# Moving the difference attention of a transformer's last layer between the products of that layer's projections

## The chip, the cores and the metric

The kernel runs on one core of one Trainium2 chip. The metric is the time of one execution in microseconds (us) on the device. Smaller is better. Three executions of the kernel before took 2349.47, 2349.73 and 2356.16 us; the median is 2349.73 us.

A core has five engines that run their own instruction streams and meet by semaphores: TensorE (PE, matrix products; its weight loads are listed as PEld), VectorE (DVE), ScalarE (ACT), GpSimd (POOL) and SyncE (SP, which issues most DMAs). Matrix products are written to PSUM, which this kernel uses as eight banks of 128 x 512 fp32 numbers, bank 0 to bank 7.

## The reference

Input `x` is 512 tokens of width 1024, all fp32. A first block of two layers is followed by a second block of one layer. The change concerns the attention of that last layer:

```python
h = rms_norm_2(x, g_attn[l])
proj = h @ w_in[l]                       # 1024 -> 3072
dq, dk, dv, sq, sk, sv = jnp.split(proj, cut, axis=-1)   # 512 columns each
dq = rms_norm_2(dq, qn_g[l])             # per head half of 64
dk = rms_norm_2(dk, kn_g[l])
lam = exp(sum(lam_q1*lam_k1)) - exp(sum(lam_q2*lam_k2)) + lambda_init
# difference attention, 4 heads, in blocks of 128 queries
probs(q, k) = softmax(where(mask, q @ k.T * scale + bias, -inf))
w = probs(q1b, k1) - lam * probs(q2b, k2)
o_da = rms_norm_2(w @ v, subln_g) * (1 - lambda_init)
# stick-breaking attention, 8 heads, on sq, sk, sv
o_sb = rms_norm_2(stick_breaking(sq, sk, sv), sb_out_g)
x = x + concatenate([o_da, o_sb]) @ w_o[l]
x = x + hier_moe(rms_norm_2(x, g_ffn), ...)   # 32 experts, top 2 of one group
```

## The kernel before

The program is written engine by engine: `tensor_program`, `scalar_program`, `vector_program` and `sync_program` each list the stages in the same order, and every wait is written out. Within an engine instructions run strictly in the written order. The tail of the dense part is: the projections of the last layer, a preparation, the difference attention (DA), the stick-breaking attention (SB), the output projection (channels `CH_2O`), and then the mixture of experts.

A dense matrix product is done in pairs of output tiles (`pe_block`), by a Strassen-like scheme of seven products. Each product is four matmuls of 128 x 256 columns, one after the other into half a bank; the program numbers the seven places `part[1]` to `part[7]`. PE writes the products in the order 1, 6, 7, 5, 2, 4, 3. `block_parts` says in which bank each lies: four banks, and which four alternates, banks 0 to 3 for even pair numbers and 4 to 7 for odd ones. The last layer's projection has 24 tiles, so 12 pairs, called pair 0 to pair 11 here (j = 0, 2, ... 22 in `pe_project`). Pair 0 is an "opening" pair, whose products are interleaved.

ACT copies product 1 out (`act_first`). DVE combines the rest. Its list for one pair, in order, is: four weight sums for the next pair (`dve_weights`, which first waits for all seven products of the previous pair), `dve_shared` (two additions, of which the second waits for the fourth product), two outputs from `part[5]`, two that wait for the sixth product, a scaling by the token norms (`dve_scaled`), then `dve_last_output`, which waits for the seventh product, and a second scaling. In that stage ACT also squares the eight tiles of dq and dk.

The preparation (`pe_2_prepare`, `act_2_prepare`, `dve_2_prepare`) sums these squares with eight matmuls against a constant (`pair_ones`), takes inverse roots on ACT, scales dq and dk on DVE, and turns dv and sv to token order by groups of four 128 x 128 transposes (`pe_turn`). Banks 6 and 7 serve as channels `ch6` and `ch7`, banks 4 and 5 as `k.turns`: a channel counts how often it was filled and emptied.

DA has 16 units n = (head, query block b), b = 0 to 3. The keys of block b are the first 128(b+1), so a unit's width grows with b. Per unit PE makes two logits matmuls, DVE adds mask and bias and finds the least (`dve_masks`, L1897), ACT takes the exponentials (`act_exps`, L1374), DVE mixes the two halves (`dve_da_mix`, L2175 to L2178), PE turns the result (`pe_da_turn`, L1070), it is copied to SBUF, PE multiplies it with the values (`pe_da_values`, L1080), and that is copied out. After each head `pe_da_store` turns the head's output back. PE walks these as a pipeline: at step s it does the logits of unit s, the turn of unit s-2, the values of unit s-3, and after b = 3 the store. The logits have two sets of banks (0, 1 and 2, 3), the turns banks 4 and 5. `pe_keep` issues matmuls without use, in places where PE would wait.

SP loads weight tiles for the dense products into a ring of six buffers as products free them, and after the ring's last tile it starts on the experts' weights (`moe_sync`, L2434 is the load of one piece).

Of the kernel before, what the change touches and what calls it, by code (L numbers as in the profile page):

```python
# [290 lines left out]
def signals(k):  # L291
# [13 lines left out]
    s.new("d_lg_done", "d_masked", "d_exp_done", "d_mixed", "d_t_done", "d_turned0", "d_turned1")  # L305
# [3 lines left out]
def buffers(k):  # L309
# [70 lines left out]
    with ExitStack() as st:  # L380
# [8 lines left out]
        k.qsq = [v[:, m, :] for v in (k.vda, k.vsb) for m in range(4)]  # L389
        k.us["2"] = quarters(k.eb, 3)  # L390
# [136 lines left out]
def block_parts(k, n):  # L527


    at = {1: 0, 6: 2, 7: 4, 5: 6, 2: 1, 4: 3, 3: 5} if n in OPENING else {1: 0, 6: 1, 7: 2, 5: 3, 2: 4, 4: 5, 3: 6}  # L530
    return {p: k.bank[4 * (n % 2) + h // 2][:, h % 2 * HT:(h % 2 + 1) * HT] for p, h in at.items()}
# [13 lines left out]
def pe_block(k, c, tile, sums, at=None, order=(0, 1, 2, 3), mid=None, among=None):  # L545
# [15 lines left out]
    if n % 2:  # L561
# [4 lines left out]
    pe.wait_ge(s["ws_ready"], 4 * (pairs_before(n) + 1))  # L566
    four = [(part[1], a11, lambda j: tile(2 * j)[:, 0:HT]), (part[6], s2, lambda j: t2[:, j, :]),
# [11 lines left out]
    else:  # L579
        for at, (bank, w, x) in enumerate(four):  # L580
            for j in range(4):
                ins = pe.matmul(bank, w[:, j, :], x(j), start=j == 0, stop=j == 3)  # L582
            ins.then_inc(s["prod_done"], 1)
            if among is not None:
                among(at)
    for j in range(4):
# [430 lines left out]
def pe_2_prepare(k):  # L1017
# [15 lines left out]


def pe_da(k):
    for step in range(len(DA) + 4):
        if step < len(DA):
            pe_da_logits(k, step)
        if 0 <= step - 2 < len(DA):
            pe_da_turn(k, step - 2)  # L1040
        if 0 <= step - 3 < len(DA):
            pe_da_values(k, step - 3)
        if 0 <= step - 4 < len(DA) and DA[step - 4][1] == NB - 1:
            pe_da_store(k, step - 4)


def pe_da_logits(k, n):
    pe, s = k.pe, k.s
    h, b = DA[n]
    if n >= 2:  # L1050
        pe.wait_ge(s["d_masked"], 2 * (n - 1))
    for a in range(2):
        r = slice(a * HD, (a + 1) * HD)
        pe.matmul(logits_bank(k, n, a)[:, 0:P * (b + 1)], k.y2[r, DQ + h, b * P:(b + 1) * P], k.y2[r, DK + h, 0:P * (b + 1)],
# [3 lines left out]
def pe_da_turn(k, n):  # L1058
    pe, s = k.pe, k.s
    h, b = DA[n]  # L1060
    if n < 2:
        pe.wait_ge(k.turns[n].emptied, k.turns[n].n)
    if n >= 2:
        pe.wait_ge(s[f"d_turned{n % 2}"], n // 2)
    if n == 0 or b == 2:
        pe_keep(k, k.bank[4 + n % 2], 5)
    pe.wait_ge(s["d_mixed"], n + 1)
    e = k.E[(2 * n) % 6]
    for j in range(b + 1):
        ins = pe.transpose(k.bank[4 + n % 2][:, j * P:(j + 1) * P], e[:, j * P:(j + 1) * P], k.const("ident"))  # L1070
# [100 lines left out]
def scalar_program(k):  # L1171
# [22 lines left out]
    act_2_prepare(k)  # L1194
    act_da(k)
# [50 lines left out]
def act_project(k, first, n, y, root):  # L1246
    for j in range(0, n, 2):
        act_first(k, first + j, y[:, j, 0:HT])
# [4 lines left out]
        if first == CH_2 and 2 <= j <= 8:  # L1253
            k.act.wait_ge(k.s["scaled"], SCALED["2"] + j)
            for t in (j - 2, j - 1):
                k.act.activation(k.qsq[t], y[:, t, :], ACT.Square).then_inc(k.s["qk_square"], 1)
# [219 lines left out]
def act_2_prepare(k):  # L1476
    act, s, y = k.act, k.s, k.y2
    act.wait_ge(s["scaled"], SCALED["end"])
    act.wait_ge(s["lam_dot"], 1)
    act.activation(k.small[:, 400:402], k.small[:, 400:402], ACT.Exp).then_inc(s["lam_exp"], 1)  # L1480
    for i in range(8):
        if i >= 2:
            act.wait_ge(s["qk_normed"], i - 1)
        act_root(k, ("qk", i), k.channels[i % 2], k.channels[i % 2].bank, k.nt[i % 2], HD)
    for b in range(NB):
        act_take(k, k.turns[b % 2], ("v_sb", b), k.vsb[:, b, :], k.turns[b % 2].bank)


def act_da(k):
    act, s = k.act, k.s  # L1490
    for step in range(len(DA) + 4):
        if step < len(DA):
            act_exps(k, step, DA[step][1], "d_masked", "d_exp_done")
        n = step - 2
        if 0 <= n < len(DA) and n % 2 == 0:
            w = P * (DA[n][1] + 1)
            if n >= 2:
                act.wait_ge(k.ch6.filled, k.ch6.at["da", n - 2])
            act.wait_ge(s["d_t_done"], n + 1)
            act.copy(k.ET[0][:, 0:w], k.bank[4][:, 0:w]).then_inc(s["d_turned0"], 1)  # L1500
        n = step - 4
        if 0 <= n < len(DA) and DA[n][1] == NB - 1:
            act_take(k, k.ch7, ("da_store", DA[n][0]), k.u[:, DA[n][0], :], k.ch7.bank)


def act_sb(k):
    for step in range(SB_STEPS):
# [11 lines left out]
        if step in O_SQUARE:  # L1519
# [3 lines left out]
            act_square(k, k.u[:, t, :])  # L1523
# [32 lines left out]
def vector_program(k):  # L1556
# [26 lines left out]
    dve_2_prepare(k)  # L1583
    dve_da(k)
# [67 lines left out]
def dve_outputs(k, c, first, second, mid=None):  # L1652
# [3 lines left out]
    dve_shared(k, c, first[:, 0:HT])  # L1656
    own.link(dve.tensor_tensor(first[:, HT:T], u2, part[5], ALU.add))
# [33 lines left out]
def dve_project(k, first, n, y, name):  # L1691
    dve, s = k.dve, k.s
    for j in range(0, n, 2):
        c = first + j
        dve_weights(k, c + 2)
        mid = (lambda: dve_fin_mean(k)) if name == "norm_a2" and j == 0 else None
        if name == "norm_a1":
# [9 lines left out]
        dve_outputs(k, c, y[:, j, :], y[:, j + 1, :], mid)  # L1707
# [181 lines left out]
def dve_masks(k, n, b, mask, done, read, free, scale, tile=wide_tile):  # L1889
# [3 lines left out]
    for a in range(2):  # L1893
# [3 lines left out]
        dve.tensor_tensor_reduce(tile(k, n, b, a), logits_bank(k, n, a)[:, 0:w], mask, -scale, 3.0e38,  # L1897
# [222 lines left out]
def dve_2_prepare(k):  # L2120
    dve, s, y, own = k.dve, k.s, k.y2, k.dve_own
    dve.wait_ge(s["scaled"], SCALED["end"])
    lam, lt = k.small[:, 400:404], k.ET[0][:, 0:P]
    lv = k.vec("lam").rearrange("p (s x) -> p s x", s=2)
    dve.wait_ge(own.sem, own.link(dve.tensor_tensor(lt, lv[:, 0, :], lv[:, 1, :], ALU.mult)))
    dve.tensor_reduce(lam[:, 0:2], lt.rearrange("p (s x) -> p s x", s=2), AX.X, ALU.add).then_inc(s["lam_dot"], 1)
    own.link(dve.tensor_scalar(k.sg, k.vec("subln"), 1.0 - LAMBDA_INIT, None, ALU.mult))
    gains = own.link(dve.tensor_scalar(k.gq, k.vec("g_qn"), SCALE, None, ALU.mult))
    dve.wait_ge(s["lam_exp"], 1)
    dve.wait_ge(own.sem, own.link(dve.tensor_tensor(lam[:, 2:3], lam[:, 0:1], lam[:, 1:2], ALU.subtract)))  # L2130
    k.lam_at = own.link(dve.tensor_scalar(lam[:, 3:4], lam[:, 2:3], LAMBDA_INIT, None, ALU.add))
# [966 lines left out]
```

## Time and profile before

| what | value |
|---|---|
| median of three runs | 2349.73 us |
| lowest, highest | 2349.47, 2356.16 us |
| span of the profiled execution | 2355.5 us |
| PE busy | 2267.2 us (96%) |
| DVE busy | 1399.5 us (59%) |
| ACT busy | 538.5 us (23%) |
| mean granted clock of PE | 0.990 |

Only the span of the profiled execution, from its first to its last instruction, is given in the profile; what its execution took in all is not. The span is 5.8 us above the median of the timed runs and 0.7 us under the slowest.

PE is busy nearly always, so what costs time is read from PE's own order of work: which instructions stand in it, and where it waits. The granted clock is a share: 1.00 is 2.4 GHz, 0.50 is 1.2 GHz.

### The profile page before, as it was taken

The numbers are of one execution on the slowest core, as the hardware profiler recorded it, in microseconds if no ns is written. First come the engines' busy times: TensorE is split into PE (matmuls) and PEld (weight loads), VectorE is DVE, ScalarE is ACT, GpSimd is POOL, SyncE is SP. The second block draws the span as 40 slices with busy tenths as digits, with TensorE's granted clock in tenths as the row PEclk, the third lists the DMA queues.
The fourth block names the chain that finished last, engine by engine and source line by source line (L and its number), as shares of the span: only waits on it lengthen the run. The fifth ranks groups of instructions, "written<-read, shape, count | busy, mean of one in ns | idle before, by whom it ended". The sixth has DMA issues, their size and how long they took to land.

```text
span 2355.5 us, 29906 instructions
## 1 busy us (share of the span) xinstructions
PE 2267.2 (96%) x11200; PEld 1649.3 (70%) x11200; DVE 1399.5 (59%) x3585; ACT 538.5 (23%) x1327; POOL 50.1 (2%) x55
## 2 busy tenths in 40 slices
PE   8988999999999999999999999999899999999998
PEld 6865678888888886557888888888656643333333
DVE  6558757665665658997665665865776532222224
ACT  2013342100010114773110000300564111111111
POOL 0000000000000000000000000000000011111010
PEclk9999899999999999999999999999999999999999
DMA  5220022222222321001222222322002899999997
GB/s 204 90 81 7 12 78 72 90 90 87 84 82 88 128 72 36 2 1 54 90 85 85 82 88 90 106 91 85 24 1 101 340 408 424 423 423 421 425 425 309
DMA packets 60208, 346.57 MB, mean 147 GB/s; under 512 B 9248, under 2 KB 10144, under 8 KB 42208
## 3 DMA queue, kind: packets, MB, share of 16 engines
q1 hardware_dynamic: 55360, 335.03, 37.9%
q0 software_dynamic: 3840, 6.46, 0.7%
q10 hardware_dynamic: 864, 3.15, 0.3%
q8 instruction: 92, 1.51, 0.3%
q14 instruction: 52, 0.43, 0.1%
HBM read 337.59 MB, written 17.30 MB: 151 GB/s over the span
## 4 chain that ended last, share of the span: by engine, by line
PE 72%; DMA 7%; DVE 5%; issue 1%; ACT 1%; DVEq 0%; POOLq 0%; ACTq 0%
PE bank L582 26%; PE bank L587 7%; PE bank L594 7%; PE bank L601 7%; DMA places<-in_experts 7%; PE bank L2627 6%; PE bank L2635 3%; PE bank L573 2%; PE bank L2587 2%; DVE exps L1897 1%; PE bank L958 1%; PE bank L943 1%; PE bank L970 1%; PE bank L1151 1%; PE bank L2600 1%
## 5 line engine op out<-in xcount | busy, mean ns | idle before, releaser
L2627 PE MATMUL bank<-places,xT 128*64 128x512 f32 x824 | 185.6, 598 | 13.9 <-DMA places<-in_experts 13.8
L2834 DVE TENSOR_SCALAR square<-bank,mt 128x256 f32<-128x256 f32 x32 | 15.5, 484 | 287.3 <-ACT rope L2739 287.3
L2627 PEld LDWEIGHTS bank<-places,xT 128*64 128x64 f32 x824 | 59.6, 138 | 134.3 <-issue 118.2
L1374 ACT ACTIVATE exps<-exps,small 128x128 f32<-128x128 f32 (+1 forms) x224 | 124.3, 559 | 99.8 <-DVE small L1897 99.2
L1649 DVE TENSOR_TENSOR third<-first,bank 128x256 f32<-128x256 f32 x106 | 44.6, 421 | 164.9 <-PE bank L582 164.2
L582 PE MATMUL bank<-u,ring 128*128 128x256 f32 x576 | 136.1, 379 | 0.0
L582 PE MATMUL bank<-h_sums,w_sum 128*128 128x256 f32 x512 | 121.0, 379 | 0.0
L582 PE MATMUL bank<-h,ring 128*128 128x256 f32 x512 | 120.9, 379 | 0.0
L582 PEld LDWEIGHTS bank<-u,ring 128*128 128x128 f32 x576 | 109.4, 190 | 15.7 <-issue 1.0
L582 PE MATMUL bank<-u_mlp,ring 128*128 128x256 f32 x480 | 113.4, 379 | 0.0
L582 PE MATMUL bank<-u_mlp_sums,w_sum 128*128 128x256 f32 x480 | 113.4, 379 | 0.0
L582 PEld LDWEIGHTS bank<-h_sums,w_sum 128*128 128x128 f32 x512 | 97.3, 190 | 13.2
L582 PEld LDWEIGHTS bank<-h,ring 128*128 128x128 f32 x512 | 97.3, 190 | 13.2
L1315 ACT ACTIVATE h<-relu 128x512 f32<-128x512 f32 x64 | 40.3, 630 | 273.7 <-DVE relu L1812 249.6
L582 PE MATMUL bank<-exps,w_sum 128*128 128x256 f32 x432 | 102.1, 379 | 0.0
L582 PEld LDWEIGHTS bank<-u_mlp,ring 128*128 128x128 f32 x480 | 91.2, 190 | 12.4
L582 PEld LDWEIGHTS bank<-u_mlp_sums,w_sum 128*128 128x128 f32 x480 | 91.2, 190 | 12.4
L2635 PE MATMUL bank<-places,square 128*64 128x512 f32 x392 | 90.0, 598 | 0.1
L582 PEld LDWEIGHTS bank<-exps,w_sum 128*128 128x128 f32 x432 | 82.1, 190 | 11.2
L1897 DVE CUSTOM_DVE_ANT_0 exps<-bank,consts 128x128 f32<-128x128 f32 (+3 forms) x168 | 73.7, 477 | 14.8 <-PE bank L943 5.8
L587 PE MATMUL bank<-u,ring 128*128 128x256 f32 x336 | 81.3, 386 | 0.0
L601 PE MATMUL bank<-u,w_sum 128*128 128x256 f32 x336 | 79.4, 379 | 0.0
(478 smaller groups left out, 4255.8 us busy)
## 6 DMA issues: line engine op xcount, KB each, us to landing
places<-in_experts SPq DMA_DIRECT2D x56, 2048.0 KB, 35.9
ring<-in_dense SPq DMA_DIRECT2D x216, 512.0 KB, 4.1
places<-in_experts SPq DMA_DIRECT2D x40, 1024.0 KB, 25.4
x<-in_experts SPq DMA_DIRECT2D x12, 1024.0 KB, 37.4
w<-in_experts SPq DMA_DIRECT2D x10, 1024.0 KB, 30.5
consts<-in_experts SPq DMA_DIRECT2D x10, 1024.0 KB, 31.4
x<-in_experts SPq DMA_DIRECT2D x4, 2048.0 KB
consts<-in_consts SPq DMA_DIRECT2D x1, 2310.5 KB, 16.7
```

The lines of the kernel that those rows point to most:

```text
L573: ins = pe.matmul(bank, w[:, j, :], x(j), start=i == 0, stop=i == 3)
L582: ins = pe.matmul(bank, w[:, j, :], x(j), start=j == 0, stop=j == 3)
L587: ins = pe.matmul(part[2], a12[:, j, :], tile(2 * j + 1)[:, 0:HT], start=j == 0, stop=j == 3)
L594: ins = pe.matmul(part[4], a22[:, j, :], t4[:, j, :], start=j == 0, stop=j == 3)
L601: ins = pe.matmul(part[3], s4[:, j, :], tile(2 * j + 1)[:, HT:T], start=j == 0, stop=j == 3)
L1315: act.activation(k.hs[q % 2][:, j + a, :], k.rc[a], ACT.Square).then_inc(s["h_ready"], 1)
L1374: act.activation(e, e, ACT.Exp, bias=neg[:, a:a + 1], scale=-1.0, accum_out=total[:, a:a + 1]).then_inc(s[done], 1)
L1649: dve.tensor_tensor(u3, u2, part[7], ALU.add).then_inc(s["shared"], 1)
L1897: dve.tensor_tensor_reduce(tile(k, n, b, a), logits_bank(k, n, a)[:, 0:w], mask, -scale, 3.0e38, ALU.add, ALU.min, neg[:, a:a + 1]).then_i ...
L2587: ins = pe.matmul(k.bank[3][a * CAP:(a + 1) * CAP, :], k.S[:, b, 0:CAP], k.htok[b][:, a * T:(a + 1) * T], start=b == 0, stop=b == NB - 1)
L2627: ins = k.pe.matmul(bank[a * CAP:(a + 1) * CAP, :], xT[:, kk % 4, kk // 4, :], w[:, (2 * (kk % 2) + a) * EH:(2 * (kk % 2) + a + 1) * EH], ...
L2635: ins = k.pe.matmul(bank[a * CAP:(a + 1) * CAP, :], hT[:, c % 2, c // 2, :], w[:, c % 2 * D + a * T:c % 2 * D + (a + 1) * T], start=c == 0 ...
```

## The change

The projections' products of the last layer all go to banks 0 to 3 (`LOW`, `block_parts`). So a pair can no longer be written while the other four banks are read, and `pe_low` adds waits: each bank waits for DVE's reads of it from the pair before. Banks 4 to 7 are free during the projections. Into the gaps between the products (after product 2, 4 and 6: `among` with part 1, 3, 5) go the matmuls of the preparation (pairs 1 to 4), the turns of dv (pair 6) and, from the last gap of pair 6 on, one step of DA in each gap: step 0 in pair 6, steps 1 to 3 in pair 7, up to steps 13 to 15 in pair 11. The steps 16 to 19, which drain the pipeline, and the turns of sv follow the projections.

DA's logits now have one set of banks (4 and 5), the turns bank 6, values and store bank 7. The exponentials get a tile of their own, `exps_da`, since `exps` holds the projections' input sums. ACT does all copies of turned units and of values (before, DVE did half of the turned ones and all values). The output of DA goes to `bias` instead of `u`. The useless matmuls of the preparation and of DA are gone.

On DVE a step is mask and least of unit s, then the mix of unit s-1. It stands in three places of a pair's list: the step of the last gap (part 5) after the next pair's weight sums, the step of the first gap (`early`) after `dve_shared`, the step of the middle gap (`mid`) after the two outputs from `part[5]`.

```diff
+    first = 0 if n in LOW else 4 * (n % 2)
+    return {p: k.bank[first + h // 2][:, h % 2 * HT:(h % 2 + 1) * HT] for p, h in at.items()}
+LOW = range(CH_2 // 2, (CH_2 + N_2) // 2)
+def pe_low(k, n, bank):
+    if n not in LOW or n - 1 not in LOW:
+        return
+    pe, s, opened = k.pe, k.s, n - 1 in OPENING
+    if bank == 0:
+        if opened:
+            pe.wait_ge(s["combined"], 2 * (n - 1) + 1)
+        else:
+            pe.wait_ge(s["shared"], 2 * pairs_before(n - 1) + 1)
+    if bank == 1:
+        pe.wait_ge(s["combined"], 2 * (n - 1) + 1)
+    if bank == 2 and opened:
+        pe.wait_ge(s["combined"], 2 * (n - 1) + 2)
+    if bank == 3:
+        pe.wait_ge(s["combined"], 2 * (n - 1) + 2)
...
+DA_STEPS = len(DA) + 4
+DA_FIRST = 6
+def da_at(i, third):
+    n = 3 * (i - DA_FIRST) + third - 2
+    return n if 0 <= n < len(DA) else None
...
+def pe_2_among(k, i, part):
+    pe, s, y = k.pe, k.s, k.y2
+    if 1 <= i <= 4 and part in (3, 5):
+        t = 2 * (i - 1) + (part == 5)
+        ch = k.channels[t % 2]
+        pe.wait_ge(s["qk_square"], t + 1)
+        pe.wait_ge(ch.emptied, ch.n)
+        ch.end(pe.matmul(ch.bank, k.const("pair_ones"), k.qsq[t], start=True, stop=True), ("qk", t))
+    if i == DA_FIRST and part in (1, 3):
+        pe.wait_ge(s["scaled"], SCALED["2"] + SQ)
+        for b in (0, 1) if part == 1 else (2, 3):
+            pe_turn(k, k.turns[b % 2], ("v_da", b), [y[:, DV + m, b * P:(b + 1) * P] for m in range(4)])
+    if part in (1, 3, 5):
+        step = da_at(i, part // 2)
+        if step is not None:
+            pe_da_step(k, step)
...
 def pe_da_logits(k, n):
-    if n >= 2:
-        pe.wait_ge(s["d_masked"], 2 * (n - 1))
+    if n:
+        pe.wait_ge(s["d_masked"], 2 * n)
...
 def dve_outputs(k, c, first, second, mid=None, early=None):
     dve_shared(k, c, first[:, 0:HT])
+    if early is not None:
+        early()
     own.link(dve.tensor_tensor(first[:, HT:T], u2, part[5], ALU.add))
...
         dve_weights(k, c + 2)
+        if name == "norm_a2" and j:
+            dve_2_sooner(k, j // 2)
+            early = lambda: dve_da_step(k, da_at(j // 2, 0))
+            mid = lambda: dve_da_step(k, da_at(j // 2, 1))
...
+def dve_2_sooner(k, i):
...
+    dve_da_step(k, da_at(i - 1, 2))
+def dve_da_step(k, step):
...
+        free = (k.s["d_t_done"], step - 1, 0) if step >= 2 else None
+        dve_masks(k, step, b, k.bf[:, h, T - P * (b + 1):T], "d_lg_done", "d_masked", free, 1.0, da_tile, da_logits)
+    if 0 <= step - 1 < len(DA):
+        dve_da_mix(k, step - 1)
+def dve_da_rest(k):
+    dve_da_step(k, len(DA) - 1)
+    dve_da_step(k, len(DA))
+    for b in (2, 3):
+        dve_take(k, k.turns[b % 2], ("v_sb", b), k.vsb[:, b, :], k.turns[b % 2].bank)
```

PE around the first product group of a late pair. Before, an odd pair follows an even one without anything between (L582, L587, L594 and L601 are the products):

```order
L582 MATMUL bank4<-u_2,ring2_16 128x256 x4
L582 MATMUL bank4<-exps_61,w_sum11_24 128x256 x4
L582 MATMUL bank5<-u_2,ring3_17 128x256 x4
L582 MATMUL bank5<-exps_61,w_sum10_23 128x256 x4
L587 MATMUL bank6<-u_2,ring2_16 128x256 x4
L594 MATMUL bank6<-exps_61,ring3_17 128x256 x4
L601 MATMUL bank7<-u_2,w_sum12_25 128x256 x4
```

Now, pair 8, with its first two gaps (L1127 are logits, L1141 turns, L1151 values):

```order
L608 MATMUL bank0<-u_2,ring2_16 128x256 x4
L608 MATMUL bank0<-exps_61,w_sum01_21 128x256 x4
L1127 MATMUL bank4<-y_2_64 128x128
L1127 MATMUL bank5<-y_2_64 128x128
L1141 MATMUL bank6<-consts_13,exps_da_72 128x128 x3
L1151 MATMUL bank7<-v_da_70,expsT_62 128x128 x2
L608 MATMUL bank1<-u_2,ring3_17 128x256 x4
L608 MATMUL bank1<-exps_61,w_sum00_20 128x256 x4
L1127 MATMUL bank4<-y_2_64 128x256
L1127 MATMUL bank5<-y_2_64 128x256
L1141 MATMUL bank6<-consts_13,exps_da_72 128x128 x4
L1151 MATMUL bank7<-v_da_70,expsT_62 128x128 x3
```

After product 2 stands step 4 (logits of unit 4, turn of unit 2, values of unit 1), after product 4 step 5.

DVE at the start of the same pair. Before, the weight sums are followed at once by the pair's own additions:

```order
L1604 TENSOR_TENSOR ring5_19<-ring4_18,ring5_19 128x4x128
L1605 TENSOR_TENSOR w_sum01_21<-w_sum00_20,ring4_18 128x512
L1607 TENSOR_TENSOR w_sum02_22<-ring4_18,w_sum01_21 128x512
L1646 TENSOR_TENSOR first1_27<-y_2_64,bank4 128x256
L1649 TENSOR_TENSOR third1_29<-first1_27,bank5 128x256
L1657 TENSOR_TENSOR y_2_64<-first1_27,bank5 128x256
```

Now (L2017 is mask and least, L2301 to L2304 the mix, L1759 and L1762 are `dve_shared`):

```order
L1720 TENSOR_TENSOR w_sum12_25<-ring4_18,w_sum11_24 128x512
L2017 ISA exps_da_72,small_3<-bank4,bias_71 128x512
L2017 ISA small_3 128x1
L2017 ISA exps_da_72,small_3<-bank5,bias_71 128x512
L2017 ISA small_3 128x1
L2301 RECIPROCAL small_3<-small_3 128x2
L2302 TENSOR_TENSOR small_3<-small_3 128x1
L2303 TENSOR_SCALAR exps_da_72<-exps_da_72,small_3 128x384
L2304 SCALAR_TENSOR_TENSOR exps_da_72<-exps_da_72,small_3 128x384
L1759 TENSOR_TENSOR first0_26<-y_2_64,bank0 128x256
L1762 TENSOR_TENSOR third0_28<-first0_26,bank1 128x256
L2017 ISA exps_da_72,small_3<-bank4,bias_71 128x128
```

DVE's step 3 (masks of unit 3, mix of unit 2) stands behind the weight sums, and step 4 behind the addition that needs product 4.

## Rows read from the trace of the kernel before

**Rows 1.** Windows: projections, preparation, DA; columns PE, PEld, DVE, ACT, POOL, PEclk, DMA

```profile
1527.26:1660.21 132.95, 132.95 (x617) 117.04 (x616) 80.24 (x153) 8.28 (x19) 0.00 (x0) 1.00 0.30 95
1660.21:1677.69 17.48, 14.23 (x57) 7.68 (x55) 10.38 (x21) 11.83 (x20) 0.00 (x0) 0.93 0.08 29
1677.69:1724.26 46.57, 39.80 (x252) 28.08 (x251) 39.53 (x152) 23.23 (x76) 0.00 (x0) 0.95 0.01 1
```

**Rows 2.** Timeline of PE: start, length, instruction, idle before; pair 11 to SB

```profile
1648.12 1.89 PE L582 MATMUL bank<-u,ring 128*128 128x256 f32 x8
...
1655.03 1.89 PE L587 MATMUL bank<-u,ring 128*128 128x256 f32 x8
...
1660.21 1.05 PE L481 MATMUL bank<-consts 128*128 128x128 f32 x8
...
1724.26 2.94 PE L1139 MATMUL bank<-y 64*128 64x384 f32 x12
```

**Rows 3.** Timeline of SP: the first load of an expert's weights

```profile
1811.15 0.43 SPq L2434 DMA_DIRECT2D w<-in_experts  x1
```

**Rows 4.** Timeline of PE in the preparation: a squares' sum and a turn

```profile
1667.52 1.02 PE L1027 MATMUL bank<-v_sb,consts 128*128 128x512 f32 x2
1668.38 0.60 PE L670 MATMUL bank<-consts,y 128*128 128x128 f32 x4
```

**Rows 5.** Timeline of PE in DA: one step with b = 3

```profile
1702.47 1.13 PE L1054 MATMUL bank<-y 64*128 64x512 f32 x4
1703.54 0.42 PE L1070 MATMUL bank<-consts,exps 128*128 128x128 f32 x2
1703.80 0.40 PE L1080 MATMUL bank<-v_da,expsT 128*128 128x128 f32 x2
1704.04 0.63 PE L1091 MATMUL bank<-consts,o_tokens 128*128 128x128 f32 x4
```

**Rows 6.** Timeline of DVE in the projections, from pair 10's last output

```profile
1648.39 0.42 DVE L1672 TENSOR_TENSOR y<-y,bank 128x256 f32<-128x256 f32 x1 [0.25 <-PE bank L601]
...
1652.18 0.42 DVE L1646 TENSOR_TENSOR first<-y,bank 128x256 f32<-128x256 f32 x1
1655.30 0.42 DVE L1649 TENSOR_TENSOR third<-first,bank 128x256 f32<-128x256 f32 x1 [2.70 <-PE bank L582]
```

**Rows 7.** Timeline of DVE in DA: steps with b = 3 and b = 0

```profile
1703.74 0.69 DVE L1897 CUSTOM_DVE_ANT_0 exps<-bank,bias 128x512 f32<-128x512 f32 x1
...
1704.97 0.16 DVE L2175 RECIPROCAL small<-small 128x2 f32<-128x2 f32 x1
...
1706.35 0.42 DVE L2158 COPY expsT<-bank 128x256 f32<-128x256 f32 x1
...
1706.88 0.28 DVE L1897 CUSTOM_DVE_ANT_0 exps<-bank,bias 128x128 f32<-128x128 f32 x1
...
1707.30 0.16 DVE L2175 RECIPROCAL small<-small 128x2 f32<-128x2 f32 x1
...
1708.88 0.28 DVE L1688 COPY o_tokens<-bank 128x128 f32<-128x128 f32 x1
```

**Rows 8.** Timeline of PE: a turn in DA that waited for the mix

```profile
1709.11 0.63 PE L1070 MATMUL bank<-consts,exps 128*128 128x128 f32 x4 [0.68 <-DVE exps L2178]
```

**Rows 9.** Timeline of ACT: in the projections, and exponentials in DA

```profile
1651.78 0.37 ACT L1218 COPY y<-bank 128x256 f32<-128x256 f32 x1 [11.71 <-PE bank L582]
...
1704.47 0.72 ACT L1374 ACTIVATE exps<-exps,small 128x512 f32<-128x512 f32 x1 [1.25 <-DVE small L1897]
```

**Rows 10.** Timeline of PE: waits of about 1.6 us, two stages earlier

```profile
179.41 1.13 PE L663 MATMUL bank<-y_ab,consts 128*128 128x512 f32 x2 [1.64 <-DVE rope L1828]
268.72 1.52 PE L481 MATMUL bank<-consts 128*128 128x128 f32 x6 [1.61 <-ACT y_ab L1243]
```

**Rows 11.** Windows of 3.40 us behind these two waits

```profile
268.72:272.12 3.40, 3.40 (x16) 3.25 (x16) 1.93 (x8) 0.00 (x0) 0.00 (x0) 0.53 0.00 0
...
179.41:182.81 3.40, 3.40 (x18) 2.26 (x20) 3.28 (x6) 0.88 (x3) 0.00 (x0) 1.00 0.05 7
```

More of the change, by code:

```diff
@@ L560, in pe_block @@
         pe.wait_ge(s["combined"], 2 * (n - 1))
-    if n % 2:
+    if n % 2 and n not in LOW:
         for ch in k.channels:
@@ L585, in pe_block @@
                 among(at)
+    pe_low(k, n, 2)
     for j in range(4):
@@ new lines, in pe_da_step, with pe_da_rest @@
+def pe_da_step(k, step):
+    if step < len(DA):
+        pe_da_logits(k, step)
+    if 0 <= step - 2 < len(DA):
+        pe_da_turn(k, step - 2)
+    if 0 <= step - 3 < len(DA):
+        pe_da_values(k, step - 3)
+    if 0 <= step - 4 < len(DA) and DA[step - 4][1] == NB - 1:
+        pe_da_store(k, step - 4)
+def pe_da_rest(k):
+    pe, s, y = k.pe, k.s, k.y2
+    pe_da_step(k, len(DA))
+    pe.wait_ge(s["scaled"], SCALED["end"])
+    pe.wait_ge(s["d_masked"], 2 * len(DA))
+    for b in (0, 1):
+        pe_turn(k, k.turns[b], ("v_sb", b), [y[:, SV + m, b * P:(b + 1) * P] for m in range(4)])
+    pe_da_step(k, len(DA) + 1)
+    for b in (2, 3):
+        pe_turn(k, k.turns[b % 2], ("v_sb", b), [y[:, SV + m, b * P:(b + 1) * P] for m in range(4)])
+    pe_da_step(k, len(DA) + 2)
+    pe_da_step(k, len(DA) + 3)
+    for ch in k.turns:
+        pe.wait_ge(ch.emptied, ch.n)
@@ L1247, in act_project @@
     for j in range(0, n, 2):
+        if first == CH_2 and da_at(j // 2 - 1, 2) is not None:
+            act_da_turned(k, da_at(j // 2 - 1, 2) - 2)
         act_first(k, first + j, y[:, j, 0:HT])
@@ L1252, in act_project @@
             act_c_among(k, j // 2)
[L1253 to L1256, printed above, removed]
+        if first == CH_2:
+            act_2_among(k, j // 2)
 def act_fin_roots(k):
@@ L1473, in act_nsa_turned, with act_2_among @@
                  k.bank[4 + a][:, 0:P * (b + 1)].rearrange("p (j t) -> p j t", t=P)).then_inc(s[f"c_turned{a}"], 1)
-def act_2_prepare(k):
+def act_2_among(k, i):
     act, s, y = k.act, k.s, k.y2
[L1478 to L1486, printed above, removed]
@@ L1489, in act_da @@
-def act_da(k):
-    act, s = k.act, k.s
[L1491 to L1503, printed above, removed]
+    if i == 1:
+        act.wait_ge(s["lam_dot"], 1)
+        act.activation(k.small[:, 400:402], k.small[:, 400:402], ACT.Exp).then_inc(s["lam_exp"], 1)
@@ new lines, in act_2_among @@
+    if 1 <= i <= 4:
+        act.wait_ge(s["scaled"], SCALED["2"] + 2 * i)
+        for t in (2 * i - 2, 2 * i - 1):
+            act.activation(k.qsq[t], y[:, t, :], ACT.Square).then_inc(s["qk_square"], 1)
+        for t in (2 * i - 2, 2 * i - 1):
+            if t >= 2:
+                act.wait_ge(s["qk_normed"], t - 1)
+            act_root(k, ("qk", t), k.channels[t % 2], k.channels[t % 2].bank, k.nt[t % 2], HD)
+    if i == DA_FIRST:
+        for b in range(NB):
+            act_take(k, k.turns[b % 2], ("v_da", b), k.vda[:, b, :], k.turns[b % 2].bank)
@@ new lines, in act_2_among, with act_da_turned @@
+    before = da_at(i - 1, 2)
+    if before is not None:
+        act_da_weights(k, before)
+    for third in range(2):
+        step = da_at(i, third)
+        if step is not None:
+            act_da_turned(k, step - 2)
+            act_da_weights(k, step)
+def act_da_turned(k, n):
+    act, s = k.act, k.s
+    if 0 <= n < len(DA):
+        w = P * (DA[n][1] + 1)
+        if n >= 2:
+            act.wait_ge(k.ch7.filled, k.ch7.at["da", n - 2])
+        act.wait_ge(s["d_t_done"], n + 1)
+        act.copy(k.ET[n % 2][:, 0:w], k.ch6.bank[:, 0:w]).then_inc(s["d_turned"], 1)
@@ new lines, in da_tile, with act_da_rest, o_source @@
+def da_tile(k, n, b, a):
+    return k.eda[:, (2 * n + a) % 4, 0:P * (b + 1)]
+def act_da_rest(k):
+    act_da_turned(k, len(DA) - 3)
+    act_da_weights(k, len(DA) - 1)
+    act_da_turned(k, len(DA) - 2)
+    act_da_weights(k, len(DA))
+    for b in (0, 1):
+        act_take(k, k.turns[b], ("v_sb", b), k.vsb[:, b, :], k.turns[b].bank)
+    act_da_turned(k, len(DA) - 1)
+    for step in (1, 2, 3):
+        act_da_weights(k, len(DA) + step)
+def o_source(k, t):
+    return k.bf[:, t, :] if t < 4 else k.u[:, t, :]
@@ L1886, in dve_index, with dve_masks @@
                 last[b] = n
-def dve_masks(k, n, b, mask, done, read, free, scale, tile=wide_tile):
+def dve_masks(k, n, b, mask, done, read, free, scale, tile=wide_tile, logits=logits_bank):
     dve, s, w = k.dve, k.s, P * (b + 1)
```

171 lines of the change are left out of this document (80 added, 91 removed).

## The prediction, made before the changed kernel ran

> **What bounds the kernel now.** I read the windows by stage first, then PE's timeline, then DVE's and ACT's in the two stages that merge. In the projections PE is busy for all of 132.95 us and DVE for 80.24 of them; ACT works 8.28 us [rows 1]. In the preparation PE is busy 14.23 of 17.48 us, in DA 39.80 of 46.57 us, while DVE works 39.53 of the 46.57 [rows 1]. So PE bounds the projections, and DVE about DA. From the end of the last product (1660.21) to the first logits of SB (1724.26) lie 64.05 us [rows 2]; this is what the change can win. What comes later follows SB at a fixed distance: SP starts the experts' loads at 1811.15 [rows 3], behind ring loads that PE's products release, so a shift of SB's start moves the end one for one. I count only up to SB.
>
> A product takes (1655.03 - 1648.12) / 4 = 1.73 us, a pair 1660.21 - 1648.12 = 12.09 us [rows 2].
>
> **PE work that moves into the projections.** Nothing of it runs in parallel to the products, since both are PE; only waits and useless matmuls can vanish.
> - Preparation: 8 sums of squares of 1668.38 - 1667.52 = 0.86 us [rows 4]: 6.9 us, pairs 1 to 4. ACT's squares and roots and DVE's scaling fit there: ACT idles 11.71 us between copies [rows 9]. No stall counted; the cover gone, a pair would wait about one root, under 1.5 us.
> - Pair 6: 16 transposes at 0.13 us (two take 1703.80 - 1703.54 = 0.26) and the logits of step 0 [rows 5]. A pair of logits of 512 columns takes 1.07 us [rows 5]; for 384, 256 and 128 I scale to 0.85, 0.64 and 0.43. Together 2.5 us.
> - Steps 1 to 15: logits as above, turns 0.13 per block, values 0.25 per block (one block 0.24), store about 0.56 [rows 5]. Four steps of a head: logits 2.99, turns 1.30, values 2.50, store 0.56, so 7.3 us. Steps 4 to 15 are three heads' worth, 22.0; steps 1 to 3 give 3.2. Sum 25.2 us.
>
> **The waits that come with it.** Each step's logits need the masks of the step before (one set of banks now), and its turn needs the mix of DVE's step before. DVE's mask part takes 1704.97 - 1703.74 = 1.23 us for b = 3 and 0.42 for b = 0, its mix 1706.35 - 1704.97 = 1.38 (384 columns) and 1708.88 - 1707.30 = 1.58 (512) [rows 7]; between them I take 0.69 and 0.96 for masks, 0.98 and 1.19 for mixes. From DVE's next instruction (1708.88) to the PE instruction that waited for it (1709.11) is 0.23 us [rows 7, 8].
>
> First gap of a pair, from the end of the pair before (time 0): DVE needs 1652.18 - 1648.12 = 4.06 us until the weight sums are done [rows 2, 6], and only then comes the step of the last gap. PE has only two products, 3.45 us. For pair 8: masks 4.06 + 1.23 + 0.23 = 5.52, so PE waits 2.07; logits to 5.95; the mix is there at 4.06 + 1.23 + 1.38 + 0.23 = 6.90, so it waits 0.95 more.
>
> Middle gap: DVE's step stands behind the addition that needs product 4, which starts 1655.30 - 1655.03 = 0.27 us after that product [rows 2, 6] and takes about 0.34. PE is at the gap at once. For pair 8: 0.27 + 0.34 + 0.42 + 0.23 = 1.26 us of wait, logits 0.64, then the mix of 1.58, so 0.94 more.
>
> Last gap: two products lie between, DVE is in time, no wait. Where b = 3, the store must wait until ACT has copied the turned unit and the values: I take 0.6 us, three times.
>
> The same walk for the five pairs, waits in the first and middle gap: pair 7 1.26 and 1.66; pair 8 3.02 and 2.20; pair 9 1.92 and 3.02; pair 10 1.66 and 1.92; pair 11 2.20 and 1.66. Sum 20.5, with the stores 22.3 us. Pairs 7 to 11 thus grow by 25.2 + 22.3 = 47.5 us, to about 21.6 us each. The new bank waits (`pe_low`) cost nothing: bank 3 needs the output that DVE starts 0.27 us after a pair's end [rows 2, 6], and PE reaches it six products later.
>
> **Behind the last product.** DVE ends its outputs (1.3 us), masks (1.23) and the mix of unit 14 (1.38): PE turns unit 14 at 4.2. The mix of unit 15 comes behind ACT's exponentials of two times 0.72 us [rows 9] at about 5.9; then turn, ACT's copies (0.6 each, of sv as well), values of four blocks (1.0), a copy, the store: SB starts near 10.8 us.
>
> **Sum.** 6.9 + 2.5 + 47.5 + 10.8 = 67.7 us, where now 64.05 stand: +3.7 us. The change wins nearly all waits and useless matmuls of preparation and drain, and pays them back as 22.3 us of new waits. For these 22.3 the bounds are 0 (DVE always ahead, as in the last gap) and about twice the value, 45 (each step waits for the whole of DVE's step, some 2.6 us by rows 7, with 0.3 around it).
>
> **The clock.** PE's granted clock falls from 2.4 to 1.2 GHz after some waits. Two waits of nearly the same length differ: behind 1.61 us of idling the next 3.40 us ran at 0.53, behind 1.64 us they ran at 1.00 [rows 10, 11]. The change makes ten places with 1.3 to 3.0 us of waiting, on a PE that was never idle in the projections (clock 1.00 [rows 1]). By the two rows about half of ten fall, at 3.40 x (1 - 0.53) = 1.6 us each: 5 x 1.6 = 8 us. Bounds: 0, and ten falls with 16 us. The preparation and DA now have falls too (0.93 and 0.95 [rows 1]), inside the 64.05.
>
> The Trainium skill, "TensorE: Matmul & The Clock Gate", section "A second HAM failure mode: psum-queue depth-cycling", says that PE idling briefly between groups of matmuls while it cycles through PSUM banks makes the clock swing between its two levels, at a cost between each burst. Taken strictly it would have every one of the ten waits fall; the two rows above agree for one wait and disagree for the other.
>
> **Result.** +3.7 + 8 = +11.7 us. The profiled span of 2355.5 would become 2367.2; the timed runs' median lies 5.8 below that span, and no row says where, so the difference goes onto the median: 2349.7 + 11.7 = 2361 us.
>
> **Rivals.**
> - DVE keeps ahead (not slower: faster). Mechanism: in the first and middle gap the masks and the mix are done when PE comes, because products, additions and steps slide against each other. Price: the 22.3 us of waits vanish, 67.7 - 22.3 - 64.05 = -18.7: 2331 us. It decides when DVE's step ends within 3.45 us of the pair's start. For it: DVE works only 80.24 of 132.95 us in the projections. Against it: the weight sums alone take 4.06, and the middle gap's step is behind product 4 by its place in the order. Half of the waits, and no fall: 2342.
> - The waits are as I say, but the clock stays up. +3.7: 2353 us. For it: the wait of 1.64 us that cost nothing. Against: some of the new stretches idle 3 us within 4.
> - Every wait drops the clock. 3.7 + 16 = +19.7: 2369 us, and more where a fall slows DVE's next release as well. For it: the wait of 1.61 us; the page's rule gives the same. Against: the other wait.
> - DVE becomes the bound outright: its work in a late pair is 80.24 / 11 = 7.3 plus three steps of about 2.2, so 13.9 us of 21.6. It isn't; I give it 2 in 100 and no line in the range.
>
> **Chances.** Forecast (waits, about half the falls) 0.42; DVE ahead, wholly or half, 0.13; clock stays up 0.30; every wait drops it 0.13; rest 0.02. 0.3% or 7 us is about what a measurement of this kernel can tell from no change: 2342.7 to 2356.8. Faster: 0.13. Same: the third case and the rest, 0.32. Slower: 0.55. Range: from the half-way case of the first rival, 2343, to somewhat over the last case with its side costs, 2375. The forecast's own range is 2355 to 2367.
>
> **What would show it.** PE's timeline of a late pair should show a wait for DVE's least (the logits) and for the mix (the turn) in the first two gaps, none in the third, and pairs of 20 to 23 us. DVE's timeline: the masks right behind the weight sums, 4.06 us after the pair's start, and idle time before the addition that needs product 4. Windows of the late pairs should show the clock under 1.00. From the last product to SB about 11 us. Pairs 1 to 4 should take 13.8 us without a wait. It is wrong if pairs 7 to 11 take under 19 us, if there are waits on banks 0 to 3 (released by DVE's outputs), or if the end doesn't follow SB's start.

## The result: 0.4% slower, as forecast

| | before | changed |
|---|---|---|
| median of five runs | 2353.61 us | 2362.96 us |
| lowest, highest | 2349.47, 2357.64 | 2361.55, 2365.10 |
| profiled span | 2355.5 us | 2360.3 us |
| ratio, 95% interval | | 1.0044 (1.0031 to 1.0057) |

The forecast was 2361 us, in a range from 2343 to 2375, and "slower" with a chance of 0.55. The first three runs of before had given 2349.7; with two more its median is 2353.6, and 27 further ones, beside e5 to e8 below, gave 2354.9. The changed kernel, run again beside those (e8), took 1.0030 times as long as before (1.0016 to 1.0045).

The two spans differ by less than the times. So I compare one stretch of PE's timeline: from the last layer's opening sum of squares (L511, start 1520.36 before) to the first logits of SB. It took 1724.26 - 1520.36 = 203.9 us before and 1729.57 - 1516.90 = 212.7 us now, 8.8 us more. Outside it the changed profile happened to be 3.5 us earlier at the opening, and from SB to the end there are 631.2 us before [rows 2] and 630.7 now.

The windows of the changed kernel: pairs 2 to 4 with the preparation, pairs 7 to 11, the rest up to SB (columns as in [rows 1]):

```profile
1535.87:1577.28 41.41, 41.41 (x181) 34.20 (x180) 28.47 (x55) 12.16 (x21) 0.00 (x0) 1.00 0.23 76
1605.45:1717.24 111.79, 92.62 (x449) 71.40 (x447) 61.01 (x181) 29.40 (x95) 0.00 (x0) 0.95 0.15 51
1717.24:1729.57 12.33, 7.97 (x46) 7.49 (x45) 6.37 (x16) 4.56 (x11) 0.00 (x0) 0.72 0.00 0
```

Three pairs with two sums of squares each take 41.41 us, 13.80 each, and PE is busy for all of it: 12.09 for the products, 1.72 for the sums, nothing for waits. Then five pairs take 111.79 us, where before they took 60.4, and PE is idle for 19 of them. The clock is below 1.00 there; before it was 1.00 [rows 1]. The pairs are uneven: from the start of one to the start of the next, pair 7 takes 18.2 us, 8 23.9, 9 25.7, 10 21.5 and 11 22.4. The prediction's sign of 20 to 23 us holds for the last two only; the mean, 22.4, lies near the 21.6 foreseen without falls of the clock.

What PE waited for from pair 7 to SB (total us, times, longest):

```profile
PE bank L1127 <- DVE small L2017: 13.1, 10, 1.8
PE bank L1141 <- DVE exps_da L2304: 8.4, 8, 4.0
PE bank L1161 <- ACT o_tokens L1312: 1.7, 4, 0.5
```

Each line says how long PE waited in all for one kind of release, how often, and the longest. There are ten waits of logits for the least, seven of turns for the mix and one long one of 4.0 us behind the last product, and four of stores. No product waited for a bank (0 to 3) that DVE still had to read.

PE's timeline of pair 8 shows the pattern (L608, L614, L621, L629 are products, L1127 logits, L1141 turns, L1151 values; in brackets the idle time before, and what ended it):

```profile
1623.76 1.89 PE L608 MATMUL bank<-u,ring 128*128 128x256 f32 x8
1625.49 1.89 PE L608 MATMUL bank<-exps,w_sum 128*128 128x256 f32 x8
1629.11 0.49 PE L1127 MATMUL bank<-y 64*128 64x128 f32 x4 [1.73 <-DVE small L2017]
1630.59 0.52 PE L1141 MATMUL bank<-consts,exps_da 128*128 128x128 f32 x3 [0.98 <-DVE exps_da L2304]
1630.94 0.96 PE L1151 MATMUL bank<-v_da,expsT 128*128 128x128 f32 x4
1631.69 3.26 PE L608 MATMUL bank<-u,ring 128*128 128x256 f32 x8
1634.79 1.89 PE L608 MATMUL bank<-exps,w_sum 128*128 128x256 f32 x8
1637.69 0.70 PE L1127 MATMUL bank<-y 64*128 64x256 f32 x4 [1.00 <-DVE small L2017]
1639.36 0.63 PE L1141 MATMUL bank<-consts,exps_da 128*128 128x128 f32 x4 [0.97 <-DVE exps_da L2304]
1639.82 0.83 PE L1151 MATMUL bank<-v_da,expsT 128*128 128x128 f32 x6
1640.49 1.89 PE L614 MATMUL bank<-u,ring 128*128 128x256 f32 x8
1642.22 1.89 PE L621 MATMUL bank<-exps,ring 128*128 128x256 f32 x8
1644.04 0.92 PE L1127 MATMUL bank<-y 64*128 64x384 f32 x4
```

The first two gaps wait, the third (1644.04) does not. The product at 1631.69 lasts 3.26 us in place of 1.89. The granted clock there is 0.50, the lower level, 1.2 GHz. A short window in that product, a wider one around it, and one in pair 9:

```profile
1632.60:1633.10 0.50, 0.50 (x3) 0.41 (x2) 0.00 (x0) 0.00 (x0) 0.00 (x0) 0.50 0.00 0
1630.20:1633.60 3.40, 3.01 (x12) 2.69 (x13) 0.57 (x2) 0.75 (x2) 0.00 (x0) 0.62 0.00 0
1661.40:1668.20 6.80, 5.82 (x21) 4.92 (x18) 3.57 (x12) 2.04 (x8) 0.00 (x0) 0.53 0.00 0
```

DVE's timeline at the start of pair 9 (which begins at 1647.67) answers to [rows 6]:

```profile
1649.01 0.68 DVE L1715 TENSOR_TENSOR w_sum<-ring 128x512 f32<-128x512 f32 x1
...
1651.05 0.69 DVE L1720 TENSOR_TENSOR w_sum<-ring,w_sum 128x512 f32<-128x512 f32 x1
1651.66 0.55 DVE L2017 CUSTOM_DVE_ANT_0 exps_da<-bank,bias 128x384 f32<-128x384 f32 x1
...
1653.39 0.48 DVE L2304 SCALAR_TENSOR_TENSOR exps_da<-exps_da,small 128x256 f32<-128x256 f32 x1
1653.80 0.41 DVE L1759 TENSOR_TENSOR first<-y,bank 128x256 f32<-128x256 f32 x1
1659.34 0.42 DVE L1762 TENSOR_TENSOR third<-first,bank 128x256 f32<-128x256 f32 x1 [5.13 <-PE bank L608]
1659.68 0.68 DVE L2017 CUSTOM_DVE_ANT_0 exps_da<-bank,bias 128x512 f32<-128x512 f32 x1
```

The masks begin 1651.66 - 1647.67 = 3.99 us after the pair (4.06 foreseen), straight behind the weight sums. The four sums alone take 1651.66 - 1649.01 = 2.65 us of that; the rest is the pair before's last output and scaling. Later DVE stands idle for 5.13 us before the addition that needs product 4 (L1762), with the masks that PE will want behind it in the list. The two engines wait for each other in turn.

### The profile page after: what moved, and what is told of

Same layout as the page of the kernel before. It is cut to its first block, busy times and chain, and to the rows that moved or that the text cites. A ratio compares the mean times of both kernels' runs of the same rounds, so it can differ in the third digit from the quotient of the medians.

```text
span 2360.3 us, 29791 instructions
## 1 busy us (share of the span) xinstructions
PE 2256.1 (96%) x11142; PEld 1640.7 (70%) x11142; DVE 1388.6 (59%) x3559; ACT 548.7 (23%) x1353; POOL 50.1 (2%) x55
## 4 chain that ended last, share of the span: by engine, by line
PE 69%; DMA 7%; DVE 7%; ACT 2%; issue 2%; SPq 0%; DVEq 0%; ACTq 0%; POOLq 0%
PE bank L608 25%; PE bank L614 7%; PE bank L621 7%; PE bank L629 7%; DMA places<-in_experts 7%; PE bank L2753 6%; PE bank L2761 3%; PE bank L597 2%; PE bank L2713 1%; PE bank L994 1%; PE bank L979 1%; DVE exps L2017 1%; PE bank L1006 1%; PE bank L2726 1%; DVE exps L2207 1%
## 5 line engine op out<-in xcount | busy, mean ns | idle before, releaser
L1762 DVE TENSOR_TENSOR third<-first,bank 128x256 f32<-128x256 f32 x106 | 44.7, 421 | 172.3 <-PE bank L608 171.6
L608 PE MATMUL bank<-u,ring 128*128 128x256 f32 x576 | 137.6, 382 | 0.0
L1443 ACT ACTIVATE exps<-exps,small 128x128 f32<-128x128 f32 (+1 forms) x192 | 106.6, 560 | 83.3 <-DVE small L2017 82.8
L608 PEld LDWEIGHTS bank<-u,ring 128*128 128x128 f32 x576 | 110.0, 192 | 16.1 <-issue 1.3
L608 PE MATMUL bank<-h_sums,w_sum 128*128 128x256 f32 x512 | 121.0, 379 | 0.0
L608 PE MATMUL bank<-h,ring 128*128 128x256 f32 x512 | 120.9, 379 | 0.0
L608 PE MATMUL bank<-u_mlp,ring 128*128 128x256 f32 x480 | 113.4, 379 | 0.0
L608 PE MATMUL bank<-u_mlp_sums,w_sum 128*128 128x256 f32 x480 | 113.4, 379 | 0.0
L608 PEld LDWEIGHTS bank<-h,ring 128*128 128x128 f32 x512 | 97.3, 190 | 13.2
L608 PEld LDWEIGHTS bank<-h_sums,w_sum 128*128 128x128 f32 x512 | 97.3, 190 | 13.2
L608 PE MATMUL bank<-exps,w_sum 128*128 128x256 f32 x432 | 102.0, 379 | 0.0
L608 PEld LDWEIGHTS bank<-u_mlp,ring 128*128 128x128 f32 x480 | 91.2, 190 | 12.4
L608 PEld LDWEIGHTS bank<-u_mlp_sums,w_sum 128*128 128x128 f32 x480 | 91.2, 190 | 12.4
L608 PEld LDWEIGHTS bank<-exps,w_sum 128*128 128x128 f32 x432 | 82.1, 190 | 11.2
L2017 DVE CUSTOM_DVE_ANT_0 exps<-bank,consts 128x128 f32<-128x128 f32 (+3 forms) x168 | 73.6, 476 | 14.6 <-PE bank L979 5.8
L614 PE MATMUL bank<-u,ring 128*128 128x256 f32 x336 | 81.2, 385 | 0.0
L1287 ACT COPY first<-bank 128x256 f32<-128x256 f32 x44 | 16.4, 372 | 275.1 <-PE bank L608 259.4
```

The lines of the kernel that those rows point to most:

```text
L614: ins = pe.matmul(part[2], a12[:, j, :], tile(2 * j + 1)[:, 0:HT], start=j == 0, stop=j == 3)
L1443: act.activation(e, e, ACT.Exp, bias=neg[:, a:a + 1], scale=-1.0, accum_out=total[:, a:a + 1]).then_inc(s[done], 1)
L1762: dve.tensor_tensor(u3, u2, part[7], ALU.add).then_inc(s["shared"], 1)
L2017: dve.tensor_tensor_reduce(tile(k, n, b, a), logits(k, n, a)[:, 0:w], mask, -scale, 3.0e38, ALU.add, ALU.min, neg[:, a:a + 1]).then_inc(s[ ...
```

## The experiments

Three theories of the waits: A, DVE's list of instructions puts the steps too late; B, the single set of logits banks makes them, whatever DVE's order; C, DVE has too much work in these pairs. "Stretch" is the time from the opening sum of squares to SB in the run's profile: 203.9 us before, 212.7 changed. "Late pairs" are pairs 7 to 11: 60.4 us before, 111.8 changed. The ratios of e1 to e4 are to 21 executions of before with a median of 2355.9 us, those of e5 to e8 to 27 with 2354.9. Stretch, late pairs and their clock are read from one profiled execution of each run.

| run | median us | ratio to before, interval | stretch | late pairs | clock in them |
|---|---|---|---|---|---|
| e1_step_first | 2352.5 | 0.9985 (0.9974 to 0.9997) | 201.7 | 101.7 | 0.97 |
| e2_step_early | 2350.4 | 0.9977 (0.9967 to 0.9987) | 197.0 | 97.2 | 1.00 |
| e3_both | 2340.6 | 0.9930 (0.9915 to 0.9945) | 188.5 | 88.5 | 1.00 |
| e4_useless | 2367.3 | 1.0045 (1.0032 to 1.0058) | 212.6 | 112.6 | 1.00 |
| e5_banks | 2355.5 | 0.9998 (0.9988 to 1.0008) | 204.0 | 60.4 | 1.00 |
| e6_prepare | 2348.6 | 0.9970 (0.9958 to 0.9982) | 197.3 | 60.4 | 1.00 |
| e7_useless_half | 2357.8 | 1.0009 (0.9999 to 1.0020) | 206.9 | 107.2 | 1.00 |
| e8_changed_again | 2362.2 | 1.0030 (1.0016 to 1.0045) | 212.5 | 111.7 | 0.95 |

**e1_step_first: the last gap's step ahead of the weight sums**

The comments in this excerpt and in that of e4 are not in the code.

```diff
         c = first + j
+        if name == "norm_a2" and j:
+            dve_da_step(k, da_at(j // 2 - 1, 2))
         dve_weights(k, c + 2)
...
-    dve_da_step(k, da_at(i - 1, 2))      # in dve_2_sooner
```

> The changed kernel, with DVE's step of a pair's last gap moved ahead of the next pair's weight sums. Theory A (DVE's list makes the waits): the waits of the first gaps, 8.4 us in the changed kernel's profile (five for the least, three for the mix), fall to under 1 us; the middle gaps keep their 9.2 us. About 8 us faster than the changed kernel, 10 where the clock's fall in pair 8 goes too: 2353 us. Theory B (one set of logits banks makes them, whatever DVE's order): the waits stay, 2363 us. Theory C (DVE is full in the late pairs): the wait moves to the weight sums or to the outputs, 2363 us.

All waits for DVE in the first gaps are gone, the middle ones stay. Up to SB (the 4.0 is the wait behind the last product, in this list and those below):

```profile
PE bank L1127 <- DVE small L2019: 6.9, 5, 1.8
PE bank L1141 <- DVE exps_da L2305: 6.3, 5, 4.0
PE bank L1161 <- ACT o_tokens L1312: 1.9, 4, 0.6
```

Late pairs 10.1 us shorter than in the changed kernel, and DVE's work is the same. A holds for the first gaps; B and C don't. The clock fell twice again: in the middle gap of pair 9 as in the changed kernel, and in pair 8 in the middle gap in place of the first.

**e2_step_early: the first gap's step ahead of the addition that needs product 4**

```diff
     dve.tensor_tensor(u2, one, part[6], ALU.add).then_inc(s["shared"], 1)
+    if between is not None:
+        between()
     dve.wait_ge(s["shared"], 2 * pairs_before(n) + 1)
     dve.wait_ge(s["prod_done"], 7 * n + 4)
     dve.tensor_tensor(u3, u2, part[7], ALU.add).then_inc(s["shared"], 1)
...
-    dve_shared(k, c, first[:, 0:HT])
-    if early is not None:
-        early()
+    dve_shared(k, c, first[:, 0:HT], early)
```

> The changed kernel, with DVE's step of the first gap moved between the two additions of dve_shared, so ahead of the one that needs product 4. Theory A: the waits of the middle gaps, 9.2 us in the changed kernel's profile, fall to under 1 us, the first gaps keep their 8.4 us, and the fall of the clock in pair 9 (2.7 us) goes: 10 to 12 us faster than the changed kernel, 2352 us. Theory B (one set of logits banks): the waits stay, 2363 us. Theory C: the wait moves to another instruction, 2363 us.

Now the middle gaps are free of waits and the first ones keep theirs:

```profile
PE bank L1127 <- DVE small L2017: 6.3, 5, 1.7
PE bank L1141 <- DVE exps_da L2304: 6.1, 4, 4.0
```

Late pairs 14.6 us shorter. In this profile the clock did not fall once in them, though pair 8's first gap waits exactly as in the changed kernel:

```profile
1624.69 0.49 PE L1127 MATMUL bank<-y 64*128 64x128 f32 x4 [1.73 <-DVE small L2017]
1626.16 0.52 PE L1141 MATMUL bank<-consts,exps_da 128*128 128x128 f32 x3 [0.98 <-DVE exps_da L2304]
```

```profile
1625.80:1629.20 3.40, 3.04 (x18) 2.82 (x19) 2.53 (x10) 1.43 (x6) 0.00 (x0) 1.00 0.00 0
```

The same waits of 1.73 and 0.98 us were followed by the low clock there and not here. What came before differs: in the changed kernel PE had also waited 1.27 and 0.16 us in the middle gap of pair 7, here not. Whether that decides is not tested.

The profile is of e2's fastest execution: 2342.3 us, with a mean granted clock of 0.994 over the whole kernel. The nine others took 2346.3 to 2351.9 us at 0.990 to 0.993, and where their clock fell is not known. So the late pairs without a fall are shown for this one execution. It also fits that e2's stretch is 15.7 us shorter than the changed kernel's, its median only 12 to 13.

**e3_both: both moves**

> Both moves of DVE's steps together. Theory A: no wait over 0.6 us in the late pairs but those of the store, pairs 8 to 11 at 17.5 to 18.5 us each, clock at 1.00 in them: 17.5 us of waits and 4 us of falls go, 2341 us, faster than the kernel before by 12 us. Theory B: 2363 us. Theory C (DVE is full: some 14 us of work in a pair that now takes 17.5 to 18): part of the waits comes back, 2345 to 2355 us.

```profile
PE bank L1141 <- DVE exps_da L2305: 4.0, 1, 4.0
PE bank L1161 <- ACT o_tokens L1312: 1.9, 4, 0.6
```

```profile
1608.80:1697.28 88.48, 86.82 (x449) 67.67 (x447) 60.86 (x181) 28.31 (x95) 0.00 (x0) 1.00 0.21 65
```

No wait for DVE is left in the late pairs, and PE is busy 86.82 of 88.48 us, with the same 61 us of DVE's work as in the changed kernel: C is out, DVE is 69% busy and in time. B is out as well: one set of logits banks is enough, if a step's masks come while PE does two products. At 0.9930 times before, this version is faster than both kernels.

**e4_useless and e7_useless_half: useless matmuls in the waits, against the clock's fall**

```diff
+    waits = step < len(DA) and (step + 2) % 3 != 2
+    if waits:
+        if step >= 3:
+            k.pe.wait_ge(k.s["d_turned"], step - 2)
+        pe_keep(k, k.bank[6], 8)            # e7: 4
     if step < len(DA):
         pe_da_logits(k, step)
+    if waits and step >= 3 and DA[step][1] < 2:
+        pe_keep(k, k.bank[6], 7)            # e7: 3
```

> The changed kernel, with useless matmuls into bank 6 where PE waits in the first and middle gaps: eight ahead of the logits, seven ahead of the turn where b is 0 or 1. The order of DVE is untouched. If falls of the clock cost what the prediction says, the waits stay as times but the clock stays at 1.00 in the late pairs: 4 us less than the changed kernel in the profile, 2359 us. If falls cost nothing because they lie in waits: 2363 us. If the useless matmuls (0.1 us each) outlast the waits: 2364 to 2367 us.

The clock stayed at 1.00 in the late pairs, but nothing was won. I had taken 0.1 us for such a matmul; the row says 1634.89 - 1633.00 = 1.89 us for eight, 0.24 each. The profile lists each of them twice (x16 for eight), so a row of x8 like that at 1660.21 [rows 2] is four of them and not eight:

```profile
1633.00 1.95 PE L481 MATMUL bank<-consts 128*128 128x128 f32 x16
1634.89 0.49 PE L1134 MATMUL bank<-y 64*128 64x128 f32 x4
```

They outlasted waits of 0.9 to 1.8 us, so PE was the late one. As a test of what the falls cost this run says nothing. With half of them:

> The changed kernel with half the useless matmuls of the run before: four ahead of the logits, three ahead of the turn, since one of them took 0.24 us and eight outlasted the waits by some 0.5 us. If the clock's falls cost what the prediction says, pairs 7 to 11 take 107 to 108 us with a clock of 1.00, in place of 111.8, and the time is 3 to 4 us under the changed kernel's in the same call. If the falls are worth nothing: the same time.

```profile
1606.10:1713.25 107.15, 100.33 (x553) 81.27 (x551) 61.04 (x181) 29.23 (x95) 0.00 (x0) 1.00 0.17 54
```

107.15 us with the clock at 1.00, against 111.7 for the changed kernel in e8: the falls cost 4.6 us there, and the medians differ by 4.4 (2357.8 and 2362.2). The changed kernel's own timeline gives the same: up to the next instruction at full clock, the slow ones of pair 8 took 1.7 us longer than their like at full clock, those of pair 9 2.9. The waits are still paid, as matmuls and as the rest of them.

**e5_banks: only banks 0 to 3**

The edit is the change's `LOW`, `block_parts` and `pe_low` in the kernel before, and the four useless matmuls of the preparation go to bank 4.

> The kernel before, with only the banks of the change: the last layer's products in banks 0 to 3, with the new waits of PE on DVE's reads; preparation and DA stay behind the projections. Theory: the new waits cost nothing, since DVE has read each bank at least 0.7 us before PE writes it again. From the opening's sum of squares to SB 203.9 us as before, time within 1 us of the kernel before. Rival: four banks in place of eight make PE wait, at least 0.5 us in each of 11 pairs, 6 us or more slower.

From pair 1's first product to the last product's end (columns as in [rows 1]):

```profile
1528.02:1660.99 132.97, 132.97 (x618) 117.11 (x617) 80.23 (x153) 8.29 (x19) 0.00 (x0) 1.00 0.30 95
```

PE was busy all the time, with the seventh products 12.09 us apart as before. The stretch is 204.0 us. The new waits of PE cost nothing.

**e6_prepare: banks and preparation, DA left behind**

The edit is e5 with the change's `pe_2_among`, `act_2_among` and `dve_2_sooner` without their DA steps; `pe_2_prepare` keeps only the turns of sv, and four useless matmuls ahead of them (L481 below).

> The kernel before, with the banks and only the preparation moved into the projections (eight sums of squares in pairs 1 to 4, the turns of dv in pair 6); DA with its two sets of logits banks follows as before. 8.7 us of PE work move in, the 17.5 us of the preparation become the turns of sv with ACT's copies, some 4 us: 5 us faster than the kernel before. If moving anything into the projections costs waits there (pairs 1 to 4 over 14.5 us): no gain.

Behind the last product only this is left before DA's first logits (L1100):

```profile
1665.52 1.05 PE L481 MATMUL bank<-consts 128*128 128x128 f32 x8
1666.99 1.09 PE L708 MATMUL bank<-consts,y 128*128 128x128 f32 x8 [0.42 <-DVE y L1784]
1668.32 1.15 PE L708 MATMUL bank<-consts,y 128*128 128x128 f32 x8 [0.24 <-ACT v_sb L1289]
1669.40 0.93 PE L1100 MATMUL bank<-y 64*128 64x128 f32 x8
```

This takes 3.9 us in place of 17.5 [rows 1]. The stretch is 6.6 us shorter than before and the median 6.3. So the preparation's move won 6.6 us, and DA's move lost 212.7 - 197.3 = 15.4. With DVE's steps in the right places DA's move wins 197.3 - 188.5 = 8.8.

**e8_changed_again: the changed kernel once more**

> The changed kernel once more, on the same chip as the other three, for a second profile. The waits are set by the lists of instructions and should come back within 0.1 us each (18.9 us in all in pairs 7 to 11); the falls of the clock (two in these pairs in the first profile) may lie elsewhere, so pairs 7 to 11 between 107 and 116 us. About 8 us slower than the kernel before.

The waits came back within 0.1 us, and so did the falls, in the first gap of pair 8 and around the middle gap of pair 9; there for 6.8 us again:

```profile
1661.40:1668.20 6.80, 5.42 (x19) 4.55 (x20) 4.27 (x16) 2.81 (x10) 0.00 (x0) 0.57 0.00 0
```

I had thought they might lie elsewhere. Between these two profiles they did not move; between kernels they do (e1).

## Why the prediction was right

- **The stretch from the last product to SB is what counts, and the end follows it.** From SB to the end: 631.2 us before, 630.7 changed, 630.4 in e3. The distance held over a shift of SB by 15 us. The other profiles have 630.0 to 632.0, and e6 633.7; what took 2.5 us more there is not known.
- **Preparation, 6.9 us in pairs 1 to 4, and pair 6, 2.5.** Measured 6.9 and 2.3, without waits.
- **PE's work of steps 1 to 15, 25.2 us.** e3's late pairs grow by 28.1 us with 1.5 of store waits, so 26.6: 1.4 too small.
- **First gaps, 10.1 us of the 20.5.** e2 against e3, both at full clock: 97.24 - 88.48 = 8.8 us. Right in place and cause (e1), 1.3 too large. One reading was wrong: the first rival's "the weight sums alone take 4.06". That is the time from the pair's start until they are done; the four sums take 2.65 us (above). The walk used the time until they are done, so its sum stands.
- **Middle gaps, 10.5 us.** e7 against e2, both at full clock: 107.15 - 97.24 = 9.9 us, 0.6 less than foreseen. Right in place and cause (e2). e7's useless matmuls may hide or add some tenths.
- **Stores, 0.6 us each.** 0.46.
- **Bank waits nothing.** e5.
- **The clock, 8 us for five falls of ten.** This term was mis-sized: two gaps of ten were followed by the low clock, 4.6 us together. That half of the waits would be followed by it was read from two rows [rows 10]. The price of 1.6 us fits the fall in pair 8 (1.7) and not that in pair 9 (2.9), where the low clock lasted twice as long. The rival of ten falls is out. So is the strict reading of what the prediction cites from the Trainium skill, "TensorE: Matmul & The Clock Gate", section "A second HAM failure mode: psum-queue depth-cycling": eight of the ten gaps with waits were not followed by the lower level. The rival with no fall in the late pairs is what e2's profile shows, but not the changed kernel's two. Why these two gaps and not the others stays open.
- **Behind the last product, 10.8 us.** 12.3, at a clock of 0.72; e3 has 11.5 at 0.85. PE turned unit 14 after 4.16 us (4.2 foreseen); what follows ran slower than the rows at full clock from which it was worked out. The prediction counted falls for the ten gaps only, none here.
- **Sum.** 6.9 + 2.3 + 51.4 + 12.3 = 72.9 against 64.05: +8.8 in the stretch, forecast +11.7. The medians gave +9.4, and +7.3 beside e8. The nearness is in part luck: the clock's and the waits' terms were together about 5.7 us too large, PE's work and the end 2.9 too small. And that 2361 lies only 2 us from the measured 2363 owes something to the base: the median of before's first three runs was 4 us under that of five, which hid the 2.3 us by which the change itself was forecast too large.
- **DVE ahead (first rival).** It did not come true for the changed kernel, but its condition was named rightly: DVE's step must end within two products, which e3 brings about by moving two calls. I gave 2331 us for it against the median of then, an 18.7 us gain; e3 gained 15.4.

## What to carry to other kernels

When work is put between the matmuls of a stage, the free share of the helping engine (DVE 60% busy) does not tell whether it fits; the place in its list does. Write down, for each thing PE will wait for, what stands ahead of it on the other engine: here four weight sums, wanted only a pair later, and one addition that waits for PE itself, made 17.5 us of waits (13.1 + 4.4) on an engine that had none there before. Split such a change in parts too: the preparation alone won 6.6 us, which DA's loss of 15.4 covered up.

## What the runs showed of the hardware that I had not expected

- Equal waits are not followed by equal clocks: 1.73 and 0.98 us of waiting in pair 8 were followed by 1.2 GHz in two profiles of the changed kernel and by 2.4 GHz in e2's, with other waits a pair earlier.
- A useless fp32 matmul of 128 x 128 takes 0.24 us (eight in 1.89), a transpose of the same size 0.13 (two in 0.26 [rows 5]). The profile lists the eight matmuls as 16 and the two transposes as 2, which fits the ratio. Eight and seven of them in each wait gained nothing (e4), four and three won 4.4 us (e7).
